# Norms of q and k stacked in one tile, and small matmuls over fewer contraction rows, in a decoder trunk on one core

## The chip, the cores and the metric

The kernel runs on one core of a Trainium2 chip. The metric is the device time of one execution in microseconds; the time of a kernel is the median of several runs.

## The reference

One inference step of a four-layer decoder trunk, for a prompt of 256 positions and 8 sample sequences of 4 positions: 288 columns in all, model width 1024. Each layer is `x += FFN/2; x += Mixer(RMSNorm(x)); x += FFN/2`; the mixers are RWKV-7 (layers 0 and 3), differential attention (layer 1) and gated DeltaNet (layer 2). What matters here is how norms per head are used:

```
def l2norm(t, eps):
    return t * lax.rsqrt(jnp.sum(t * t, axis=-1, keepdims=True) + eps)
...
    q = l2norm(qkv_c[..., :H * DK].reshape(B, T, H, DK), 1e-6) * (DK ** -0.5)
    k = l2norm(qkv_c[..., H * DK:2 * H * DK].reshape(B, T, H, DK), 1e-6)
...
    o = rmsnorm(o, p['norm_w']) * jax.nn.silu(z.astype(f32).reshape(B, T, H, DV))
```

RWKV-7 normalises its key per head of 64 and its output per head (mean and variance); attention and DeltaNet normalise their output per head of 128. Attention adds a bias that depends on the distance of query and key, from a table of 32 buckets.

## The kernel before

Activations lie with features on partitions: eight pieces of 128 features (`CH` = 8) by 288 columns (`NT`). Weights stream through a ring of four slots. Large products are made in three reduced-precision products (`three_products`, lines 911 to 913: high by high, low by high, high by low), 8 x 3 = 24 matmuls per piece of 128 output features; ScalarE makes the high part of a weight piece, VectorE the low part. Each engine has its own hand-written program; semaphores order them, and `after(s)` waits for the next count of one.

A norm per head is made in four steps. TensorE sums squares over the features of a head with a 0/1 matrix as weights (`heads64` or `heads128`, 16 columns: two rows per head of 128, one per head of 64), accumulating over the pieces into 16 rows of a bank. ScalarE takes the root into `rms`. VectorE takes the reciprocal into `rinv`. TensorE spreads the 16 rows of `rinv` over 128 partitions again with the 0/1 matrix `spread64`, 128 columns per piece, and VectorE multiplies. Before the change the spreading matmul contracts over all 128 partitions; `spread64` is zero below row 16.

Where this stands:
- RWKV output norm: line 1210 spreads, VectorE's lines 2795 and 2797 use the result piece by piece.
- RWKV key norm: `own_rows` builds 16 rows (line 2803 on VectorE for the first chunk, 3279 on GpSimd for the others), line 1228 spreads them with `parity`, five times a stage, between the chunk's other matmuls.
- `head_norms` (lines 1835 and 1845): output norm of attention and DeltaNet. Between the two, `keep_clock` runs two matmuls on a constant.
- DeltaNet, `gdn`: the loop over c = 0 to 31 makes q, k, v and the gate. Behind the 24 products of each c from 8 to 23 stands one sum-of-squares matmul (line 1651): j = 0 to 7 for q into bank 7, j = 8 to 15 for k into bank 6, each into 16 rows. Behind c = 25, 26 and 27 stand 6, 6 and 4 spreading matmuls (line 1660), j < 8 from `rinv` and j >= 8 from `kinv`, into banks 4 to 7 in turn; from j = 4 on each waits until VectorE (line 3073) has used the bank. ScalarE takes the two roots (2395, 2396), VectorE the two reciprocals (3067, 3068), the second of which releases TensorE.
- Attention, samples' bias: line 1471 (33 rows by 8 columns), then eight matmuls of line 1475 from `rel_rows` and the one-hot `sample{i}`, both zero below row 33, then page transposes (line 1487).

A float32 matmul appears in the trace as two records, each with its weight load (PEld).

Of the kernel before, what the change touches and what calls it, by code (L numbers as in the profile page):

```python
# [8 lines left out]
DEC_B, DEC_T = 8, 4  # L9
NS = DEC_B * DEC_T  # L10
NT = SEQ + NS
CH = D // 128
# [20 lines left out]
def constant_table():  # L33
# [49 lines left out]
    wide = np.arange(CH * 128)[None, :]  # L83
    put("spread64", (np.arange(RH)[:, None] == wide // DE))
    put("heads128", (np.arange(94)[None, :] // 2 == 23) & (m >= 0))
# [56 lines left out]
def program(nc, t, stages):  # L142
# [5 lines left out]
    with ctx:  # L148
        def sb(name, shape, dt=f32):
            return ctx.enter_context(nc.sbuf_tensor(name, shape, dt))  # L150
# [47 lines left out]
        prm = sb("prm", [128, 512])  # L198
        kinv = sb("kinv", [128, NT])
        banks = ctx.enter_context(nc.psum_tensor("banks", [128, 8, 512], f32))  # L200
# [116 lines left out]
        def W(i):  # L317
            return work[:, i]
# [65 lines left out]
        MK_BANK, MB_BANK = ((6, 7), (2, 3)), ((3, 0), (0, 1))  # L384
        own_inverse = work[:, XM0_, :, :].rearrange("p c n -> p (c n)")

# [183 lines left out]
        pageT = [atok_flat[:, 1024 * i:1024 * i + 1024] for i in range(2)]  # L570
        rel_rows = atok_flat[:, REL_AT:REL_AT + 1024].rearrange("p (a i r) -> p a i r", a=2, i=DEC_T)
        q_apart = atok_flat[:, REL_AT + 1024:REL_AT + 3072].rearrange("p (h b n) -> p h b n", h=AH, b=DEC_B)
# [300 lines left out]
        def _(pe):  # L873
            pe.sem_inc(half_done, 2 * SLOTS)

            pe.wait_ge(first_in, 32)
            pe.wait_ge(consts_set, 5)
            nc.tensor.transpose(bank[0][:, 0:N_NORM], prm_rows[0:N_NORM, 0, :], ident[0:N_NORM, 0:N_NORM]).then_inc(prm_transposed, 1)
# [95 lines left out]
            def rwkv(s, j):  # L974
# [232 lines left out]
                for c in range(CH):  # L1207
                    if c >= 5:
                        after(og_ready)
                    nc.tensor.matmul(bank[OUT_SPREAD_BANK[c]][:, 0:NT], const("spread64")[:, 128 * c:128 * c + 128], rinv[:, :],  # L1210
                                     start=True, stop=True).then_inc(mean_raw, 1)
# [13 lines left out]
            def spread_inverse(i):  # L1225

                t, n, own = own_part(i)
                nc.tensor.matmul(bank[SPREAD_BANK[i]][:, 0:CH * n], const("parity"), own,
                                 start=True, stop=True).then_inc(rk_sum, 1)
# [215 lines left out]
            def attention(s):  # L1445
# [27 lines left out]
                for a in range(2):  # L1473
                    for i in range(DEC_T):
                        last = nc.tensor.matmul(bank[(7, 5)[a]][:, 0:SK], rel_rows[:, a, i, :], acon_at(f"sample{i}"),
                                                start=(i == 0), stop=(i == DEC_T - 1))
                    last.then_inc(sbias_raw, 1)
# [130 lines left out]
            def gdn(s):  # L1608
# [23 lines left out]
                for c in range(32):  # L1632
# [14 lines left out]
                    if 8 <= c < 24:  # L1647
                        j = c - 8
                        at = 46 - 2 * (j % 8)
                        after(qk_squared)  # L1650
                        last = nc.tensor.matmul(bank[7 - j // 8][0:RH, 0:NT], const("heads128")[:, at:at + RH], W(GO_)[:, j % 8, :],
                                                start=(j % 8 == 0), stop=(j % 8 == 7), skip_group_check=True)
                        if j == 15:
                            last.then_inc(qk_ssq, 1)
                    if c == 25:
                        after(qk_ready)
                    for j in {25: range(0, 6), 26: range(6, 12), 27: range(12, 16)}.get(c, ()):
                        if j >= 4:
                            after(qk_ready)
                        nc.tensor.matmul(bank[4 + j % 4][:, 0:NT], const("spread64")[:, 128 * (j % 8):128 * (j % 8) + 128],  # L1660
                                         (rinv, kinv)[j // 8][:, :], start=True, stop=True).then_inc(ks_raw, 1)
                    if c in (28, 29):
# [168 lines left out]
            def head_norms(src, at, spread_bank, meanwhile=lambda: None):  # L1831

                for c in range(CH):
                    after(sub_squared)
                    last = nc.tensor.matmul(bank[at][0:RH, 0:NT], const("heads128")[:, 46 - 2 * c:62 - 2 * c], W(src)[:, c, :],
                                            start=(c == 0), stop=(c == CH - 1))
                last.then_inc(sub_ssq, 1)
                meanwhile()
                keep_clock(spread_bank[0], 2)
                after(sub_rms)  # L1840
                after(og_ready)
                for c in range(CH):
                    if spread_bank[c] in spread_bank[:c]:
                        after(og_ready)
                    nc.tensor.matmul(bank[spread_bank[c]][:, 0:NT], const("spread64")[:, 128 * c:128 * c + 128], rinv[:, :],
                                     start=True, stop=True).then_inc(mean_raw, 1)
# [167 lines left out]
        def _(act):  # L2014
# [61 lines left out]

            act.wait_ge(consts_set, 5)
            after = follow(act)
# [250 lines left out]
            def gdn(s):  # L2329
# [64 lines left out]
                after(qk_ssq)  # L2394
                nc.scalar.activation(rms[0:RH, :], bank[7][0:RH, 0:NT], ACT.Sqrt, bias=eps_col[0:RH, 0:1])
                nc.scalar.activation(kinv[0:RH, :], bank[6][0:RH, 0:NT], ACT.Sqrt, bias=eps_col[0:RH, 0:1]).then_inc(qk_rms, 1)
                convolved(23)
# [123 lines left out]
        def _(dve):  # L2521
# [278 lines left out]
            def own_rows(i):  # L2800

                t, n, own = own_part(i)
                return TT(own[0:RH].rearrange("p (c n) -> p c n", n=n), rinv[0:RH, t].unsqueeze(1).broadcast_to([RH, CH, n]),
                                         const("own_head", RH).unsqueeze(2).broadcast_to([RH, CH, n]), ALU.mult)
# [54 lines left out]
            def attention(s):  # L2859
# [24 lines left out]
                for q in range(8):  # L2884
# [3 lines left out]
                    if q == 2:  # L2888
# [6 lines left out]
                        link(V.memset(rel_rows, 0.0))  # L2895
                        rr = rel_rows[0:BUCKETS + 1].rearrange("p a i (h b q) -> p a i h b q", h=4, b=DEC_B)
                    if q == 4:
# [92 lines left out]
            def gdn(s):  # L2990
# [75 lines left out]
                after(qk_rms)  # L3066
                V.reciprocal(rinv[0:RH, :], rms[0:RH, :])
                V.reciprocal(kinv[0:RH, :], kinv[0:RH, :]).then_inc(qk_ready, 1)

# [205 lines left out]
        def _(pool):  # L3275
            def own_rows(i):

                span, n, own = own_part(i)
                return nc.gpsimd.tensor_tensor(own[0:RH].rearrange("p (c n) -> p c n", n=n),
                                               rinv[0:RH, span].unsqueeze(1).broadcast_to([RH, CH, n]),  # L3280
                                               const("own_head", RH).unsqueeze(2).broadcast_to([RH, CH, n]), ALU.mult)
# [3 lines left out]
            for i, e in enumerate((EPS, 1e-24, 64e-5, 1e-5)):  # L3285
                nc.gpsimd.memset(eps_col[:, i:i + 1], e).then_inc(consts_set, 1)
            nc.gpsimd.memset(kinv[:, :], 1.0).then_inc(consts_set, 1)
            for src, i0, k, p0, n in row_loads[1:]:
# [275 lines left out]
```

## Time and profile before

| | |
|---|---|
| median of 3 runs | 2921.92 us (2921.31 to 2927.31) |
| the profiled execution | 2921.92 us, its span 2920.2 us |
| mean granted TensorE clock | 0.986 of full speed |
| TensorE matmuls busy | 2814.5 us, 96% of the span |
| VectorE busy | 1699.9 us, 58% |
| ScalarE busy | 1176.5 us, 40% |
| GpSimd busy | 255.5 us, 9% |

Times of a place are microseconds from the start of the span. A matmul's duration in a record includes its latency; matmuls follow each other faster than that, so starts tell the pace. The DeltaNet stage lies between about 1630 and 1919 us, attention between 996 and 1190, the RWKV stages between 245 and 560 and between 2365 and 2680.

### The profile page before, as it was taken

How to read it: one execution, taken by the hardware profiler on the slowest of the kernel's cores; microseconds unless marked ns; L12 is line 12 of the kernel's file. 1: busy time of each engine (PE TensorE's matmuls, PEld its weight loads, DVE VectorE, ACT ScalarE, POOL GpSimd, SP SyncE). 2: the span in 40 equal slices, each digit the busy share in tenths (PEclk: the TensorE clock that was granted, in tenths of full speed). 3: DMA queues.
4: the chain of work that ended last, by engine and by line, in shares of the span. 5: the costliest groups of instructions: out<-in, count | busy, mean ns of one | idle time of the engine just before them, and what ended most of it. 6: DMA issues, size and time to landing. Idle time of an engine off the chain costs nothing.

```text
span 2920.2 us, 63483 instructions
## 1 busy us (share of the span) xinstructions
PE 2814.5 (96%) x28153; PEld 2615.4 (90%) x28153; DVE 1699.9 (58%) x2572; ACT 1176.5 (40%) x1835; POOL 255.5 (9%) x334
## 2 busy tenths in 40 slices
PE   7999988999999997999999998999999999889998
PEld 7997778899999985999999888789999977788997
DVE  5646465765565546765564674456556465656654
ACT  4434333444444334544443563234344343334442
POOL 1001011100000201000000110410000010111001
PEclk9999999999999998999999999899999999999999
DMA  7443401553644654444544433254454444115531
GB/s 249 148 143 126 155 8 33 149 172 119 204 154 136 238 188 174 144 155 144 185 145 134 155 125 93 67 173 147 143 186 154 141 150 133 14 33 149 166 126 56
DMA packets 349205, 402.68 MB, mean 138 GB/s; under 512 B 31210, under 2 KB 303999, under 8 KB 348573
## 3 DMA queue, kind: packets, MB, share of 16 engines
q1 hardware_dynamic: 337696, 360.58, 38.6%
q0 software_dynamic: 11312, 39.25, 4.4%
q8 instruction: 151, 2.47, 0.4%
q14 instruction: 46, 0.38, 0.0%
HBM read 385.22 MB, written 14.57 MB: 137 GB/s over the span
## 4 chain that ended last, share of the span: by engine, by line
PE 88%; DVE 8%; ACT 2%; issue 1%; DMA 1%; POOL 0%; SPq 0%; DVEq 0%; ACTq 0%; POOLq 0%
PE banks L911 23%; PE banks L913 22%; PE banks L912 22%; PE banks L944 2%; PE banks L1077 2%; PE banks L1318 2%; PE banks L1290 1%; PE banks L1025 1%; DVE h L2539 1%; PE banks L1914 1%; PE banks L1782 1%; PE banks L901 1%; PE banks L1487 1%; PE banks L1399 1%; PE banks L1333 0%
## 5 line engine op out<-in xcount | busy, mean ns | idle before, releaser
L2554 DVE TENSOR_TENSOR w_lo<-ring,w_hi 128x2048 fp32r<-128x2048 f32 (+1 forms) x304 | 611.5, 2012 | 412.3 <-ACT w_hi L2085 412.1
L911 PE MATMUL banks<-h_hi,w_hi 128*128 128x288 f32 x2816 | 837.8, 298 | 7.4 <-DVE h_lo L2546 6.8
L912 PE MATMUL banks<-h_hi,w_lo 128*128 128x288 f32 x2816 | 831.7, 295 | 0.0
L913 PE MATMUL banks<-h_lo,w_hi 128*128 128x288 f32 x2816 | 828.8, 294 | 0.0
L2085 ACT CAST w_hi<-ring 128x2048 fp32r<-128x2048 f32 (+1 forms) x304 | 511.4, 1683 | 586.2 <-PE banks L913 555.8
L911 PEld LDWEIGHTS banks<-h_hi,w_hi 128*128 128x128 f32 x2816 | 528.4, 188 | 10.6 <-issue 6.1
L913 PEld LDWEIGHTS banks<-h_lo,w_hi 128*128 128x128 f32 x2816 | 531.4, 189 | 0.0
L912 PEld LDWEIGHTS banks<-h_hi,w_lo 128*128 128x128 f32 x2816 | 529.7, 188 | 0.4
L911 PE MATMUL banks<-hid_hi,w_hi 128*128 128x288 f32 x1408 | 416.1, 296 | 0.0
L912 PE MATMUL banks<-hid_hi,w_lo 128*128 128x288 f32 x1408 | 415.4, 295 | 0.0
L913 PE MATMUL banks<-hid_lo,w_hi 128*128 128x288 f32 x1408 | 414.3, 294 | 0.0
L913 PEld LDWEIGHTS banks<-hid_lo,w_hi 128*128 128x128 f32 x1408 | 265.1, 188 | 0.0
L912 PEld LDWEIGHTS banks<-hid_hi,w_lo 128*128 128x128 f32 x1408 | 264.3, 188 | 0.0
L911 PEld LDWEIGHTS banks<-hid_hi,w_hi 128*128 128x128 f32 x1408 | 263.9, 187 | 0.0
L2503 ACT CAST hid_hi<-work 128x288 fp32r<-128x288 f32 x176 | 76.1, 433 | 398.2 <-DVE work L3247 398.2
L3298 POOL TENSOR_TENSOR h<-h 128x288 f32<-128x288 f32 x65 | 80.4, 1237 | 1719.0 <-ACT h L2038 918.4
L3240 DVE TENSOR_TENSOR work<-banks,rinv 128x288 f32<-128x288 f32 x176 | 80.4, 457 | 155.5 <-PE banks L913 155.5
L912 PE MATMUL banks<-h_hi,ring_lo 128*128 128x288 f32 x448 | 133.4, 298 | 0.0
L3249 DVE TENSOR_TENSOR hid_lo<-work,hid_hi 128x288 fp32r<-128x288 f32 x176 | 80.7, 458 | 87.9 <-ACT hid_hi L2503 87.9
L944 PE MATMUL banks<-work,ring 128*128 128x288 f32 x384 | 94.0, 407 | 0.5 <-DVE work L3204 0.5
L944 PEld LDWEIGHTS banks<-work,ring 128*128 128x128 f32 x384 | 72.7, 190 | 20.9 <-DVE work L3204 1.0
L912 PEld LDWEIGHTS banks<-h_hi,ring_lo 128*128 128x128 f32 x448 | 85.6, 191 | 0.2
(582 smaller groups left out, 4143.9 us busy)
## 6 DMA issues: line engine op xcount, KB each, us to landing
ring<-in_ffn_w_gate SPq DMA_DIRECT2D x88, 1024.0 KB, 5.5
ring<-in_ffn_w_up SPq DMA_DIRECT2D x88, 1024.0 KB, 8.0
ring<-in_ffn_w_down SPq DMA_DIRECT2D x64, 768.0 KB, 4.7
ring<-in_ffn_w_down SPq DMA_DIRECT2D x64, 640.0 KB, 5.9
ring<-in_rwkv_w_rkv SPq DMA_DIRECT2D x24, 1024.0 KB, 6.7
ring<-in_gdn_w_in SPq DMA_DIRECT2D x16, 1024.0 KB, 6.9
ring<-in_attn_w_qkv SPq DMA_DIRECT2D x12, 1024.0 KB, 7.3
ring<-in_rwkv_w_o SPq DMA_DIRECT2D x8, 1024.0 KB, 6.2
```

The lines of the kernel that those rows point to most:

```text
L911: nc.tensor.matmul(out, w_hi_k, x_hi_k, start=start, stop=False)
L912: nc.tensor.matmul(out, w_lo_k, x_hi_k, start=False, stop=False)
L913: return nc.tensor.matmul(out, w_hi_k, x_lo_k, start=False, stop=stop)
L944: last = nc.tensor.matmul(bank[(d0 + d) % 8][:, 0:NT], w[:, k, 128 * (d % 4):128 * (d % 4) + 128], src[:, k, :], start=(k == 0), stop=(k = ...
L1077: last = nc.tensor.matmul(bank[d % 4][:, 0:NT], w[:, k, 128 * (d % 4):128 * (d % 4) + 128], W(XM1_)[:, k, :], start=(k == 0), stop=(k == C ...
L1318: last = nc.tensor.matmul(bank[(XT_BANK if w else XY_BANK)[g]][to, 64 * q:64 * q + 64], y if w else xt, xt if w else y, start=True, stop=True)
L2085: nc.scalar.copy(w_hi[e][:, 0:k, :], raw).then_inc(w_hi_ready, 1)
L2503: nc.scalar.copy(hid_hi[:, 2 * u + e, :], prod[:, e, :]).then_inc(act_hi_ready, 1)
L2554: nc.vector.tensor_tensor(w_lo[e][:, 0:k, :], raw, w_hi[e][:, 0:k, :], ALU.subtract).then_inc(w_lo_ready, 1)
L3240: nc.vector.tensor_tensor(silu[:, e, :], bank[2 * e][:, 0:NT], rinv[:, :], ALU.mult)
L3249: nc.vector.tensor_tensor(hid_lo[:, f, :], prod[:, e, :], hid_hi[:, f, :], ALU.subtract).then_inc(act_lo_ready, 1)
L3298: nc.gpsimd.tensor_tensor(h[:, c, :], h[:, c, :], h[:, other, :], ALU.add).then_inc(presummed, 1)
```

## The change

In DeltaNet the sums of squares of q and k go into one bank, q's in rows 0 to 15, k's in rows 32 to 47: all sixteen matmuls of line 1651 have 48 columns of weights and form one accumulation. One root and one reciprocal over 48 rows replace two of each over 16, and the tile `kinv` with its initial fill is gone. `spread64` holds its pattern a second time from row 32. The spreading matmuls read 16 rows of weights and of `rinv`: from row 0 for q, from row 32 for k.

The other matmuls with zero rows are cut to the rows that hold something: 16 for the output norms (1210, 1845) and `parity` (1228), 33 for the samples' bias (1475).

```diff
-    put("spread64", (np.arange(RH)[:, None] == wide // DE))
+    put("spread64", (np.arange(48)[:, None] % 32 == wide // DE))
...
-        kinv = sb("kinv", [128, NT])
...
-        own_inverse = work[:, XM0_, :, :].rearrange("p c n -> p (c n)")
+        own_inverse = work[0:RH, XM0_, :, :].rearrange("p c n -> p (c n)")
...
-        rel_rows = atok_flat[:, REL_AT:REL_AT + 1024].rearrange("p (a i r) -> p a i r", a=2, i=DEC_T)
+        rel_rows = atok_flat[0:BUCKETS + 1, REL_AT:REL_AT + 1024].rearrange("p (a i r) -> p a i r", a=2, i=DEC_T)
...
-                    nc.tensor.matmul(bank[OUT_SPREAD_BANK[c]][:, 0:NT], const("spread64")[:, 128 * c:128 * c + 128], rinv[:, :],
+                    nc.tensor.matmul(bank[OUT_SPREAD_BANK[c]][:, 0:NT], const("spread64", RH)[:, 128 * c:128 * c + 128], rinv[0:RH, :],
...
-                nc.tensor.matmul(bank[SPREAD_BANK[i]][:, 0:CH * n], const("parity"), own,
+                nc.tensor.matmul(bank[SPREAD_BANK[i]][:, 0:CH * n], const("parity", RH), own,
...
-                        last = nc.tensor.matmul(bank[(7, 5)[a]][:, 0:SK], rel_rows[:, a, i, :], acon_at(f"sample{i}"),
+                        last = nc.tensor.matmul(bank[(7, 5)[a]][:, 0:SK], rel_rows[:, a, i, :], acon_at(f"sample{i}", BUCKETS + 1),
...
-                        at = 46 - 2 * (j % 8)
+                        at = 46 - 32 * (j // 8) - 2 * (j % 8)
                         after(qk_squared)
-                        last = nc.tensor.matmul(bank[7 - j // 8][0:RH, 0:NT], const("heads128")[:, at:at + RH], W(GO_)[:, j % 8, :],
-                                                start=(j % 8 == 0), stop=(j % 8 == 7), skip_group_check=True)
+                        last = nc.tensor.matmul(bank[7][0:48, 0:NT], const("heads128")[:, at:at + 48], W(GO_)[:, j % 8, :],
+                                                start=(j == 0), stop=(j == 15), skip_group_check=True)
...
-                        nc.tensor.matmul(bank[4 + j % 4][:, 0:NT], const("spread64")[:, 128 * (j % 8):128 * (j % 8) + 128],
-                                         (rinv, kinv)[j // 8][:, :], start=True, stop=True).then_inc(ks_raw, 1)
+                        r = slice(32 * (j // 8), 32 * (j // 8) + RH)
+                        nc.tensor.matmul(bank[4 + j % 4][:, 0:NT], const("spread64")[r, 128 * (j % 8):128 * (j % 8) + 128],
+                                         rinv[r, :], start=True, stop=True).then_inc(ks_raw, 1)
...
-                    nc.tensor.matmul(bank[spread_bank[c]][:, 0:NT], const("spread64")[:, 128 * c:128 * c + 128], rinv[:, :],
+                    nc.tensor.matmul(bank[spread_bank[c]][:, 0:NT], const("spread64", RH)[:, 128 * c:128 * c + 128], rinv[0:RH, :],
...
-                nc.scalar.activation(rms[0:RH, :], bank[7][0:RH, 0:NT], ACT.Sqrt, bias=eps_col[0:RH, 0:1])
-                nc.scalar.activation(kinv[0:RH, :], bank[6][0:RH, 0:NT], ACT.Sqrt, bias=eps_col[0:RH, 0:1]).then_inc(qk_rms, 1)
+                nc.scalar.activation(rms[0:48, :], bank[7][0:48, 0:NT], ACT.Sqrt, bias=eps_col[0:48, 0:1]).then_inc(qk_rms, 1)
...
-                V.reciprocal(rinv[0:RH, :], rms[0:RH, :])
-                V.reciprocal(kinv[0:RH, :], kinv[0:RH, :]).then_inc(qk_ready, 1)
+                V.reciprocal(rinv[0:48, :], rms[0:48, :]).then_inc(qk_ready, 1)
...
-            nc.gpsimd.memset(kinv[:, :], 1.0).then_inc(consts_set, 1)
```

TensorE and ScalarE wait for four counts of `consts_set` instead of five. The fill of `rel_rows` covers its 33 rows.

## Rows read from the trace of the kernel before

**Rows 1.** The page, chain that ended last: share of the span by engine.

```profile
PE 88%; DVE 8%; ACT 2%; issue 1%; DMA 1%; POOL 0%; SPq 0%; DVEq 0%; ACTq 0%; POOLq 0%
```

**Rows 2.** The chain in order of time, DeltaNet, 1734 to 1775: start, us, what.

```profile
1739.84 1.13 DVE ring_lo L2996
1740.98 1.85 DVE rinv L3067
1742.83 1.82 DVE kinv L3068
1744.70 0.77 PE banks L1660 x2
```

**Rows 3.** Timeline, 1735 to 1775: start, us, what, in brackets idle before and releaser.

```profile
1740.19 0.48 ACT L2396 ACTIVATE kinv<-banks,eps_col 16x288 f32<-16x288 f32 x1
...
1742.84 0.29 PE L913 MATMUL banks<-h_lo,gdn_w_hi 128*128 128x288 f32 x1
...
1744.69 2.24 PEld L1660 LDWEIGHTS banks<-rinv,consts 128*128 128x128 f32 x10 [1.80 <-DVE kinv L3068]
```

**Rows 4.** Timeline, 1757 to 1760, the four spreads behind c = 27.

```profile
1757.21 0.29 PE L913 MATMUL banks<-h_lo,gdn_w_hi 128*128 128x288 f32 x1
...
1757.34 2.10 PE L1660 MATMUL banks<-kinv,consts 128*128 128x288 f32 x8
...
1759.41 0.29 PE L912 MATMUL banks<-h_hi,ring_lo 128*128 128x288 f32 x1
```

**Rows 5.** Groups by form, VectorE: line, operation, form, count, busy us, mean ns.

```profile
L2532 DVE RECIPROCAL rinv<-rms 128x288 f32<-128x288 f32 x13 | 25.4, 1951 | 12.4 <-ACT rms L2031 12.3
```

**Rows 6.** Timeline of TensorE's weight loads, 270 to 273.5, line 1025.

```profile
271.49 0.78 PEld L1025 LDWEIGHTS banks<-work,ring 128*128 128x128 f32 x4 [0.38 <-ACT work L2139]
272.66 0.30 PEld L1025 LDWEIGHTS banks<-work,ring 32*128 32x128 f32 x4 [0.39 <-ACT work L2141]
273.34 0.30 PEld L1025 LDWEIGHTS banks<-work,ring 64*128 64x128 f32 x4 [0.39 <-issue]
```

**Rows 7.** Timeline of TensorE, 1676.2 to 1678, one sum of squares.

```profile
1676.37 0.29 PE L913 MATMUL banks<-h_lo,gdn_w_hi 128*128 128x288 f32 x1
1676.59 0.66 PE L1651 MATMUL banks<-work,consts 128*16 128x288 f32 x2
...
1677.42 0.30 PE L912 MATMUL banks<-h_hi,ring_lo 128*128 128x288 f32 x1
```

**Rows 8.** The chain in order of time, attention, 1015 to 1030.

```profile
1021.08 4.08 PE banks L1475 x16
1025.16 1.75 PE banks L1487 x16
```

**Rows 9.** The chain in order of time, attention, 1160 to 1180.

```profile
1169.91 4.12 PE banks L1845 x16
1174.03 3.18 PE banks L956 x24
```

**Rows 10.** Timeline of TensorE, 1895 to 1899; the chain, RWKV, 532 to 545.

```profile
1896.45 2.94 PE L944 MATMUL banks<-work,ring 128*128 128x288 f32 x11 [0.55 <-DVE work L3204]
...
535.60 0.46 DVE work L2797
536.05 0.38 DVE work L2795
```

**Rows 11.** Groups by form, weight loads of 16, 32 and 64 columns.

```profile
L1651 PEld LDWEIGHTS banks<-work,consts 128*16 128x16 f32 x32 | 1.8, 94 | 2.6 <-issue 2.6
L1012 PEld LDWEIGHTS banks<-work,ring 128*32 128x32 f32 x32 | 1.8, 110 | 0.0
L992 PEld LDWEIGHTS banks<-work,ring 128*64 128x64 f32 x64 | 8.3, 136 | 8.2 <-issue 2.2 <-DVE work L2630 1.2
```

**Rows 12.** Timeline of GpSimd, 0 to 12.

```profile
1.17 0.34 POOL L3287 MEMSET kinv<- 128x288 f32 x1
```

**Rows 13.** Windows, TensorE: window, length, busy (count), granted clock, DMA share, GB/s.

```profile
267.10:279.40 12.30, 12.18 (x67) 1.00 0.50 171
1163.20:1167.20 4.00, 3.98 (x17) 1.00 0.00 0
1785.30:1792.20 6.90, 6.00 (x123) 0.51 0.66 191
1850.20:1853.60 3.40, 3.40 (x30) 0.51 1.02 295
```

More of the change, by code:

```diff
@@ L876, in _ @@
             pe.wait_ge(first_in, 32)
-            pe.wait_ge(consts_set, 5)
+            pe.wait_ge(consts_set, 4)
             nc.tensor.transpose(bank[0][:, 0:N_NORM], prm_rows[0:N_NORM, 0, :], ident[0:N_NORM, 0:N_NORM]).then_inc(prm_transposed, 1)
@@ L2075, in out_high @@
                         high_part(unit_base[s + 1], c // 2 - 2)
-            act.wait_ge(consts_set, 5)
+            act.wait_ge(consts_set, 4)
             after = follow(act)
@@ L2802, in own_rows @@
                 t, n, own = own_part(i)
-                return TT(own[0:RH].rearrange("p (c n) -> p c n", n=n), rinv[0:RH, t].unsqueeze(1).broadcast_to([RH, CH, n]),
+                return TT(own.rearrange("p (c n) -> p c n", n=n), rinv[0:RH, t].unsqueeze(1).broadcast_to([RH, CH, n]),
                                          const("own_head", RH).unsqueeze(2).broadcast_to([RH, CH, n]), ALU.mult)
@@ L2895, in attention @@
                         link(V.memset(rel_rows, 0.0))
-                        rr = rel_rows[0:BUCKETS + 1].rearrange("p a i (h b q) -> p a i h b q", h=4, b=DEC_B)
+                        rr = rel_rows.rearrange("p a i (h b q) -> p a i h b q", h=4, b=DEC_B)
                     if q == 4:
@@ L3278, in own_rows @@
                 span, n, own = own_part(i)
-                return nc.gpsimd.tensor_tensor(own[0:RH].rearrange("p (c n) -> p c n", n=n),
+                return nc.gpsimd.tensor_tensor(own.rearrange("p (c n) -> p c n", n=n),
                                                rinv[0:RH, span].unsqueeze(1).broadcast_to([RH, CH, n]),
```

## The prediction

> **What bounds the kernel now.** I began with the last chain of the page: TensorE holds 88% of it, VectorE 8% [rows 1]. An edit counts, then, where it moves TensorE's next instruction. The change touches small matmuls between the big products, so I went from the chain to each of its places and asked: is TensorE waiting there, or are its matmuls back to back?
>
> In the delta-rule stage it waits once. After the 24 products of c = 25 the chain leaves TensorE: VectorE takes the reciprocal of q's norms (1740.98 us, 1.85 us) and of k's (1742.83, 1.82), and only then do the spreading matmuls start, at 1744.70 [rows 2]. Their weight load sat 1.80 us behind the k reciprocal; the product before them started at 1742.84, and with the products' pitch of 0.13 us TensorE could have gone on at 1742.97 [rows 3]. So the hole is 1744.70 - 1742.97 = 1.73 us. Later, at c = 27, matmuls of the same line have no hole: last product 1757.21, first spread 1757.34, and after eight records the second product of c = 28 at 1759.41 [rows 4]. (One float32 matmul is two records.) Taking off the slot of one product, the eight fill 1757.34 to 1759.28, 0.2425 us each, nothing lost on entering or leaving.
>
> **The wait that goes.** One root over 48 rows replaces two over 16. ScalarE loses a 0.48 us activation [rows 3]; VectorE's first reciprocal starts behind its own split of weights (1739.84, 1.13 us), not behind the second root [rows 2, 3], so this is worth nothing at that point. The second reciprocal goes. One over 128 rows takes 1.95 us [rows 5] against 1.85 on the chain for 16 [rows 2], so 48 rows cost what 16 do. It is ready at 1742.83, and TensorE's load followed the old one's end at once: ready about 1742.9, just before TensorE needs it. The whole 1.73 us goes, and what is late next is TensorE itself. Everything behind is on the chain or waits for it, so it shifts along. **-1.73.**
>
> **The price of another shape in the array.** The change also cuts the rows that matmuls contract over: 16 instead of 128 for the spreads, 33 for the samples' bias. Does a shape change cost? In the RWKV stage one line runs in groups of 128, 32 and 64 rows: its weight loads begin at 271.49, 272.66 and 273.34 [rows 6]. The 128-row group is two matmuls, four records: 4 x 0.2425 = 0.97 of 1.17 us, 0.20 over. The 32-row group has two matmuls in two different row strips, which can overlap: 0.68 = 2 x 0.2425 + 0.20. So I take 0.20 us per change of shape. A second place agrees roughly: the 16-column matmuls between products take from 1676.50 (1676.37 + 0.13) to 1677.29 (1677.42 - 0.13), 0.79 us for 0.485 of work, 0.30 for entering and leaving [rows 7]. I take the larger. The lower bound is zero, as in [rows 4], should contraction rows not count as a shape.
>
> The Trainium skill, "TensorEngine Tiling (Array Packing)", Key Properties, speaks against this edit: changing the tiling mode drains TensorE. It gives no price; from the lone-matmul latency of "TensorE: Matmul & The Clock Gate", Single matmul latency, 398 extra cycles at 2.4 GHz, I get an estimate of 0.166 us a change, so 1.33 instead of 1.60 us in the sum below.
>
> Where new shape changes are on the chain:
> - spreads at c = 25, 26, 27: three entries, three exits. Rows 0 to 15 and 32 to 47 are one shape in two strips. 6 x 0.20 = **+1.20**. At c = 26, j = 7 and j = 8 are in different strips and banks; one matmul's record may hide: **-0.24** (bounds 0 and -0.49).
> - attention, samples' bias: its eight matmuls run straight into the transposes [rows 8]; it was entered from a 33x8 shape already. One exit: **+0.20**.
> - attention's head norms: the 16 records run straight into the output projection [rows 9]. The entry lies in the wait for the reciprocal. One exit: **+0.20**.
> - hidden: after the delta-rule head norms TensorE waits 0.55 us for VectorE [rows 10], which covers 0.20; without that cover it would be +0.20. In both RWKV stages the spreads are paced by VectorE, whose two operations per piece fill the time (0.46 + 0.38) [rows 10]; without it, +0.20 a stage. The five `parity` matmuls a stage stand between shapes of 64 rows or columns, so no change is added.
>
> **The wider norm sums.** Sixteen matmuls go from 16 to 48 columns. The load of 16 columns takes 94 ns, of 32 110 ns, of 64 136 ns [rows 11]; between the last two, 48 is about 124. The first load of each insertion is exposed, since the shape changes: 16 x 0.03 = **+0.48** (bounds: none exposed 0, both 0.96). The streamed columns stay 288. These products are back to back, so this moves the whole of c = 8 to 25, the reciprocal with it.
>
> **At nothing.** The `kinv` fill on GpSimd (0.34 us at 1.17) [rows 12] is away from TensorE's start, which the first weights set. Fewer semaphore counts, a fill of 33 rows rather than 128, the freed bank and the freed tile move nothing. No DMA is added or moved.
>
> **Sum:** -1.73 + 1.20 - 0.24 + 0.20 + 0.20 + 0.48 = +0.11 us. Ends of the unknowns: shape changes and loads free, -1.73 - 0.49 = -2.2; nothing hidden, both loads exposed, and the three covered exits paid: -1.73 + 1.20 + 0.40 + 0.96 + 0.60 = +1.4. The profiled execution took 2921.92 us around a span of 2920.2, and is also the median. 2921.92 + 0.11 = **2922.0 us**.
>
> **Rivals.**
> *The clock falls in the narrow stretches (slower).* Five stretches of about 4 us (bias, four head norms) would keep one eighth or a quarter of the rows at work. If the granted clock falls to 1.2 GHz after one for the shortest half-clock stretch seen, 3.4 us at 0.51 [rows 13], TensorE loses 1.7 us; five times, 8.5 us: 2930.4. It decides from four on. Against it: 12.3 us of the mixed 64-, 128- and 32-row line, and 4 us with only 16 columns, all at 1.00 [rows 13]. But in the first, strips worked side by side; 16 rows alone for 4 us is not in the trace. 7%. The skill ("TensorE: Matmul & The Clock Gate", Part 1) names busyness as what the gate watches, not rows; by that the clock stays.
>
> *The next weights are not loaded ahead (slower).* In one strip a load might have to wait for the matmul before it: 0.19 us more per record. Paid by 32 records at c = 25 to 27, 16 in the bias, 32 in the attention and delta-rule head norms: 80 x 0.19 = 15.2 us, 2937. It decides from about a third of that. Against it: four 32-row loads, two to a strip, are done in 0.30 us [rows 6]. 4%.
>
> *The clock does better (faster).* The same wait gone, and half-clock stretches behind it shrink, as the one at 1785.3 [rows 13]: 6.9 us at 0.51, a loss of 3.4. The removed hole is not the idle just before it, so I see only the shift of times that may do this. -1.73 and two such, -6.8: with the costs above about 2916. 4%.
>
> *The merge brings what it says, the rows are free (faster by less than can be told).* -1.73 - 0.24 + 0.48 = -1.5: 2920.4. This is inside no change; so are all mixtures. With the forecast, 85%.
>
> **How the numbers follow.** About 0.2%, 5.8 us, is what a measurement of this kernel can tell from no change. Forecast and its near mixtures 85%, slower 11%, faster 4% (the faster case rounded up to 5%, the forecast down to 84%). The range takes the bounds -2.2 and +1.4 and on each side the clock: one half-clock stretch less (-1.7), two more (+3.4): 2918.0 to 2926.7.
>
> **What the changed profile would show.** The reciprocal of 48 rows at 1.9 us and no second; the wait of the c = 25 spreads gone or under 0.3 us. At c = 27, from last product to first spread 0.2 us more than 0.13, and as much on leaving; if these gaps are not there, the shape price fails and the time is nearer 2920. The 48-column loads at about 124 ns, 0.82 us an insertion. The granted clock at 1.00 in all four head norms and the bias; if it is not, the first rival. A pitch of 0.43 in place of 0.24 us in the 16-row records would be the second. Wrong too if VectorE, not TensorE, were late at c = 25 through something I don't see.

## The result, and the profile after

The changed kernel took 2939.36 us (median of 8 runs, 2933.63 to 2949.81), the kernel before 2925.16 in the same session (8 runs, 2920.72 to 2930.21). The ratio is 1.0059, 95% interval 1.0045 to 1.0075: slower. A ratio here and below compares all undisturbed executions on record of both kernels (14 of the changed one), so it need not be the quotient of the two medians, 1.0049 here. The profiled execution took 2942.88 us around a span of 2941.2, 21.0 us more than before, with a mean granted clock of 0.977 (before 0.986). In this version the lines of the change moved by one: products 910 to 912, norm sums 1650, bias 1470 and 1474, output projection 955 and 959; 1660 and 1845 are the same.

The page's chain is still TensorE's, and its share rose from 88% to 89% [rows 1]:

```profile
PE 89%; DVE 7%; ACT 2%; issue 1%; DMA 1%; POOL 0%; SPq 0%; DVEq 0%; ACTq 0%; POOLq 0%
```

So no other engine took over. The first thing to look at is the place where the wait was. The timeline of TensorE around c = 25 (start, us, what, in brackets the idle time before):

```profile
1757.21 0.29 PE L912 MATMUL banks<-h_lo,gdn_w_hi 128*128 128x288 f32 x1
...
1757.43 1.75 PEld L1660 LDWEIGHTS banks<-rinv,consts 16*128 16x128 f32 x8 [0.16 <-issue]
```

The hole of 1.73 us [rows 3] is gone: the last product's slot ends at 1757.21 + 0.13 = 1757.34, and the spreads' first weights load at 1757.43. The change did what it says there. One sum of squares between the products, same view:

```profile
1690.25 0.29 PE L912 MATMUL banks<-h_lo,gdn_w_hi 128*128 128x288 f32 x1
...
1690.48 0.69 PE L1650 MATMUL banks<-work,consts 128*48 128x288 f32 x2
...
1691.33 0.30 PE L911 MATMUL banks<-h_hi,ring_lo 128*128 128x288 f32 x1
```

From 1690.38 to 1691.20 it is 0.82 us, against 0.79 with 16 columns [rows 7]. Both are the sizes of the prediction.

Now the chain in order of time, attention, at the samples' bias and the transposes, and then at the head norms and the output projection:

```profile
1023.41 6.64 PE banks L1474 x16
1030.06 3.60 PE banks L1486 x16
...
1178.90 5.22 PE banks L1845 x16
1184.12 5.40 PE banks L955 x24
```

Before, these four steps took 4.08, 1.75, 4.12 and 3.18 us [rows 8, 9]. The narrow matmuls are longer, and so are the wide ones behind them, which the change doesn't touch. The windows view says why (window, length, TensorE's busy time with the number of its records, granted clock, DMA share, GB/s); first the kernel before at its norms and bias in RWKV, attention, attention, DeltaNet, RWKV:

```profile
533.80:544.00 10.20, 9.68 (x51) 1.00 0.62 202
1021.00:1031.20 10.20, 10.13 (x101) 1.00 0.69 250
1169.90:1176.70 6.80, 6.79 (x38) 1.00 0.00 0
1891.80:1898.60 6.80, 6.25 (x25) 1.00 0.65 186
2653.60:2663.80 10.20, 9.65 (x51) 1.00 0.60 195
```

The changed kernel at the same places, and behind the spreads at c = 25, 26 and 27:

```profile
536.10:542.90 6.80, 6.80 (x22) 0.54 0.70 228
1024.20:1034.40 10.20, 10.20 (x46) 0.53 0.49 187
1181.20:1188.00 6.80, 6.80 (x24) 0.54 0.00 0
1761.50:1764.90 3.40, 3.40 (x18) 0.58 0.02 5
1768.30:1771.70 3.40, 3.40 (x16) 0.58 0.00 0
1775.10:1778.50 3.40, 3.40 (x15) 0.58 1.00 343
1908.20:1915.00 6.80, 6.25 (x16) 0.54 0.31 92
2672.80:2683.00 10.20, 10.20 (x35) 0.53 0.51 167
```

TensorE is busy in all of them and gets through fewer records: 24 against 38 in 6.80 us at the attention norm, 46 against 101 in 10.20 us at the bias. The clock had fallen to its lower level, 1.2 GHz. (These windows begin about 0.5 us ahead of the fall, which is why they read 0.53 to 0.58; moved on by that much, each of them reads 0.50.) The fall comes inside the narrow run and lasts beyond it: the norms' first narrow records start at 534.42, 1178.90, 1905.81 and 2671.45 us, and the clock is at half from 536.6, 1181.8, 1908.8 and 2673.4 on, 1.9 to 3.0 us later. The first rival of the prediction is there, at each of its five places (the bias and the four output norms), and also between and behind the spreads, where the prediction had not looked for it. Where the norms' time went shows in the stretch from each output-norm reciprocal to the next norm's first sum: before 37.25, 34.96, 45.14 and 37.25 us, after 38.95, 38.29, 48.18 and 40.48: +11.3 us. The bias stretch adds 4.35 us (5.90 to 10.25). Together 15.6 of the 21.0 us between the two spans.

The spreads lose time too, and it comes back behind them. Between the groups of c = 25 and 26, and of 26 and 27, the same run of products takes 4.44 us in the changed kernel (1761.32 to 1765.76, 1768.68 to 1773.12) and took 2.90 before (1748.22 to 1751.12). But from there to the DeltaNet norm the kernel before has half-clock stretches of its own, as the one at 1785.3 [rows 13], and the changed kernel has fewer. The windows from c = 28 to the norm's reciprocal, the kernel before, then the changed one:

```profile
1763.00:1889.70 126.70, 116.65 (x2052) 0.91 0.23 67
1779.20:1903.70 124.50, 114.17 (x2065) 0.95 0.23 67
```

From the second product of c = 28 to that reciprocal it is 130.3 us before (1759.41 to 1889.71) and 128.0 after (1775.74 to 1903.72). This is one execution of each.

### The profile page after: what moved, and what is told of

It reads as the page before. It is cut to its first block, busy times and chain, and to the rows that moved or that the text cites. A ratio compares the mean times of both kernels' runs of the same rounds, so it can differ in the third digit from the quotient of the medians.

```text
span 2941.2 us, 63480 instructions
## 1 busy us (share of the span) xinstructions
PE 2838.1 (96%) x28153; PEld 2633.9 (90%) x28153; DVE 1697.8 (58%) x2571; ACT 1176.0 (40%) x1834; POOL 256.6 (9%) x333
## 4 chain that ended last, share of the span: by engine, by line
PE 89%; DVE 7%; ACT 2%; issue 1%; DMA 1%; POOL 0%; SPq 0%; DVEq 0%; ACTq 0%; POOLq 0%
PE banks L910 23%; PE banks L912 22%; PE banks L911 22%; PE banks L943 2%; PE banks L1076 2%; PE banks L1317 2%; PE banks L1289 1%; PE banks L1024 1%; DVE work L2629 1%; DVE work L2721 1%; DVE h L2538 1%; PE banks L1486 1%; PE banks L1914 1%; PE banks L900 1%; PE banks L955 1%
```

## The experiments

Three theories stood at the start. A: few contraction rows lower the clock. B: the changes of shape cost more than 0.20 us. C: the merge itself (wider sums, one reciprocal) costs. All ratios below are to the kernel before on the same chip, with 95% intervals; the median of before was 2922.07, 2922.63, 2924.52 and 2922.55 us in the four sessions.

### First session: the merge apart from the rows, and the number of rows

**merge_full_rows**: the merge alone. Every matmul contracts over 128 rows; k's spread table is built by GpSimd in a free part of `h`.

```
+ if c == 12: memset(hflat[:, 0:1024], 0.0); tensor_copy(hflat[32:48, 0:1024], const("spread64", RH))
- ... const("spread64")[r, 128 * (j % 8):128 * (j % 8) + 128], rinv[r, :]
+ spread = const("spread64")[:, 128 * j:128 * j + 128] if j < 8 else hflat[:, 128 * j - 1024:128 * j - 896]
+ ... spread, rinv[:, :]
```

> The merge alone (norm sums of q and k in one bank, one root, one reciprocal), with every matmul contracting over all 128 rows as before; k's spreads take their 128-row 0/1 matrix from a table that GpSimd builds in a free part of h. Clock theory (few contraction rows lower the granted clock): no new half-clock stretches behind the spreads of c = 25 to 27, the bias and the output norms; the time is 1 to 2 us below the kernel before, which its measurement can hardly tell (ratio 0.999 to 1.001). Rival (the merge itself, its wider sums, costs the time): ratio about 1.006, as with the whole change.

**rows16_all**, **rows64_all**, **rows96_all**: the kernel before with all cut matmuls (norms, spreads, parity, bias) over 16, 64 or 96 rows (the bias 33, 64, 96), no merge.

```
- const("spread64")[:, ...], rinv[:, :]          + const("spread64", R)[:, ...], rinv[0:R, :]
- const("parity"), own                           + const("parity", R), own
- acon_at(f"sample{i}")                          + acon_at(f"sample{i}", max(R, 33))
```

> The row cuts alone, no merge: 16 rows in the spreads, the parity matmuls and the output norms, 33 in the bias. Clock theory: half-clock stretches behind each of the groups, ratio 1.005 to 1.009, as slow as the whole change or slower by the 1 to 2 us that the merge gives. Rival (the merge costs it): ratio 1.000 to 1.001.

> The same matmuls cut to 64 rows instead of 16. The array's shape changes here as with 16 rows. Shape theory (entering and leaving another shape, or loads not made ahead, costs the time): as slow as with 16 rows, ratio 1.005 or more. Clock theory, if the number of rows at work is what counts: clearly less than with 16, ratio under 1.003, fewer or no new half-clock stretches; if any cut of rows does it, as with 16.

> The same matmuls cut to 96 rows. Clock theory by the number of rows: no new half-clock stretches, ratio 0.999 to 1.001. Shape theory: 96 rows need the full shape, so also 0.999 to 1.001; together with the 64-row run this tells whether shape or rows decide. If it is as slow as with 16 rows, both fall.

| kernel | us | ratio | interval |
|---|---|---|---|
| merge_full_rows | 2921.19 | 0.9992 | 0.9983 to 1.0001 |
| rows16_all | 2942.43 | 1.0061 | 1.0048 to 1.0074 |
| rows64_all | 2925.71 | 1.0015 | 1.0006 to 1.0024 |
| rows96_all | 2924.10 | 1.0006 | 0.9997 to 1.0014 |

The merge doesn't cost; theory C falls. The row cuts alone, with nothing else of the change, give all of the loss (1.0061 against 1.0059). At 64 rows most of it is gone. Yet the price of the shape is the same there: at c = 27 of rows64_all, by the reckoning of [rows 4], the eight records fill 2.33 us where it was 1.94, and over 16 rows they fill 2.34 (second session). So B can't be the main cause. In rows64_all the windows over the bias and the first norms read:

```profile
533.80:551.00 17.20, 16.57 (x109) 1.00 0.23 74
1020.00:1035.00 15.00, 14.93 (x188) 1.00 0.79 262
```

In merge_full_rows one reciprocal over 48 rows takes what the prediction said (timeline; 1.95 for 128 rows [rows 5]):

```profile
1744.90 1.94 DVE L3069 RECIPROCAL rinv<-rms 48x288 f32<-48x288 f32 x1
```

### Second session: which place, and 32 rows

Each kernel is the one before with one cut: **rows32_all** as above with R = 32; **only_norms16** the four output norms; **only_spreads16** the spreads at c = 25 to 27; **only_bias33** the bias.

```
only_norms16:   + const("spread64", 16)[:, 128 * c:128 * c + 128], rinv[0:16, :]
only_spreads16: + const("spread64", 16)[:, 128 * (j % 8):...], (rinv, kinv)[j // 8][0:16, :]
only_bias33:    + acon_at(f"sample{i}", 33)
```

> The same matmuls as in the cut to 16 rows, but over 32 rows (the bias stays at 33). The array's shape is the same as with 16 rows, one strip; only the number of rows at work is doubled. Shape theory (one strip of 32, whatever is in it, costs it): ratio 1.005 to 1.007, as with 16. Row-count theory, in proportion: between 16 rows (1.0061) and 64 rows (1.0015), about 1.003 to 1.005.

> The kernel before with only the spreads of the four output norms (two RWKV, attention, gated DeltaNet) cut to 16 rows. Clock theory: a half-clock stretch behind each of the four, none behind the bias and c = 25 to 27; 6 to 12 us, ratio 1.002 to 1.004, the costs of the places adding up to the 18 us of the full cut. Shape theory: four exits of 0.2 us, ratio under 1.001.

> The kernel before with only the spreads at c = 25 to 27 of gated DeltaNet cut to 16 rows (from rinv and kinv, no merge). Three groups of 1.5 to 3 us between full-row products. Clock theory: short half-clock stretches among c = 25 to 28, 2 to 6 us, ratio 1.001 to 1.002. Shape theory: six changes of 0.2 us, 1.2 us, not told from nothing.

> The kernel before with only the samples' bias in attention cut to 33 rows. 33 rows need the 64-row shape. In the changed kernel the clock was at half from inside this group on. If 33 rows are few enough, half clock for 7 to 10 us there, 3 to 5 us, ratio 1.001 to 1.002; if what stood in the full change was set off by something else, nothing, 0.999 to 1.001.

| kernel | us | ratio | interval |
|---|---|---|---|
| rows32_all | 2938.57 | 1.0050 | 1.0037 to 1.0063 |
| only_norms16 | 2936.76 | 1.0047 | 1.0033 to 1.0061 |
| only_spreads16 | 2923.40 | 1.0000 | 0.9991 to 1.0010 |
| only_bias33 | 2927.60 | 1.0018 | 1.0007 to 1.0030 |

The norms are worth 13.7 us (0.47% of 2922.6; by the interval 10 to 18), the bias 5.3 (2 to 9), the spreads nothing that can be measured. For the norms that is more than the clock theory had expected, for the spreads less. 32 rows lie where both theories of that run allow it. The bias in its own kernel, in the windows view:

```profile
1023.50:1030.30 6.80, 6.80 (x38) 0.50 0.41 150
```

The windows of only_norms16 at its four norms show the same fall as the changed kernel:

```profile
539.50:546.30 6.80, 6.78 (x23) 0.55 0.58 186
1177.80:1184.60 6.80, 6.80 (x22) 0.55 0.00 0
1904.80:1911.60 6.80, 6.25 (x16) 0.55 0.39 114
2666.00:2676.20 10.20, 10.20 (x33) 0.53 0.55 181
```

Its four stretches from reciprocal to next norm sum grew by 1.9, 3.4, 3.0 and 3.3 us, 11.6 of the 14.8 us between the spans; the other 3.2 us arose before the first norm, which the edit can't reach.

only_spreads16 gives the price of a shape change without the merge. Timeline at c = 27:

```profile
1758.52 0.29 PE L913 MATMUL banks<-h_lo,gdn_w_hi 128*128 128x288 f32 x1
...
1758.75 0.51 PE L1660 MATMUL banks<-kinv,consts 16*128 16x288 f32 x1
...
1761.12 0.29 PE L912 MATMUL banks<-h_hi,ring_lo 128*128 128x288 f32 x1
```

Eight records fill 1758.65 to 1760.99, 2.34 us, where before it was 1.94 [rows 4]: 0.40 more for entering and leaving, 0.10 of it ahead of the first record. That is the prediction's 2 x 0.20. It also leaves no room for 0.19 us more per record, which would be 1.5 us here: the rival of weights not loaded ahead falls. At c = 26 the twelve records fill 3.31 us, 0.40 more than the 2.91 before; in the changed kernel, where they stand in two strips, they fill 2.66 us at the full clock (1765.76 + 0.13 to 1768.68 - 0.13). So the second strip saves 0.65 us.

### Third session: parity, a repeat, and two attempts to hold the clock

**only_parity16**: `const("parity", 16)` and 16 rows of `own_inverse`, nothing else. **merge_full_again**: merge_full_rows once more. **norms16_filled**: only_norms16 with a 128-row matmul behind each narrow one, whose result nobody reads. The edit reached the two RWKV norms alone; attention and DeltaNet stayed as in only_norms16, which its expectation doesn't say. **change_with_strips4**: the changed kernel, norm sums written in four copies (112 columns), so that the spreads of c = 0, 1, 2, 3 read four row strips in turn; the bias over 128 rows.

```
norms16_filled:
+ nc.tensor.matmul(bank[0][:, 0:NT], ident, consts[:, 0:NT], start=True, stop=True)
change_with_strips4:
+ bank[at][0:112, 0:NT], const("heads4x")[:, 14 - 2 * c:126 - 2 * c]
+ const("spread64")[32 * (c % 4):32 * (c % 4) + RH, ...], rinv[32 * (c % 4):32 * (c % 4) + RH, :]
```

> The kernel before with only the parity matmuls of the RWKV key norm cut to 16 rows: five a stage, 0.5 to 2 us each, far apart. The other three places measured 1.0047, 1.0018 and 1.0000 alone, all four together 1.0061; so this one should be nothing, 0.999 to 1.001, by the clock theory and by the shape theory alike. If it is over 1.002, the parts do not add up and something else acts.

> The merge with all matmuls over 128 rows a second time, since it is the candidate for beating both kernels: 0.9992 [0.9983, 1.0001] the first time. From the trace the wait of 1.73 us at c = 25 goes and the wider loads cost 0.4 to 0.5 us: ratio 0.9995, that is 0.9986 to 1.0004; clearly faster only if the interval stays below 1.

> The cut of the output norms' spreads to 16 rows (1.0047 alone), with one matmul on a constant over all 128 rows and 288 columns behind each narrow one in the two RWKV norms and in attention (not in gated DeltaNet). Its result is overwritten and not used. It adds 8 x 0.49 = 3.9 us of TensorE work per place, which is on the path in attention and almost wholly under VectorE's 0.86 us per piece in RWKV. Clock theory: full clock behind the RWKV and attention norms again, still half behind the DeltaNet norm; about 3.9 + 2 x 1 + 3 = 9 us over the kernel before, so less than with the narrow ones alone: ratio 1.002 to 1.0035. Shape theory: more work and more shape changes, so slower than without it: ratio over 1.006.

> The whole change, but the four output norms' sums are made in four copies (112 columns, rows 0, 32, 64 and 96), the root and reciprocal taken over 112 rows, and the spreads of pieces c and c + 4 read their 16 rows from strip c mod 4, so that up to four run side by side; the bias is back at 128 rows. The merge and the narrow spreads at c = 25 to 27 stay. Theory that few rows at work in the array at one time lower the clock: four times 16 rows is 64 at once, so the clock behind the norms is held or falls less, unless TensorE then idles longer because the spreads are over sooner; ratio 0.999 to 1.002. Theory that the narrow shape as such does it: half clock behind the norms as before, ratio about 1.004.

| kernel | us | ratio | interval |
|---|---|---|---|
| only_parity16 | 2923.19 | 0.9998 | 0.9989 to 1.0007 |
| merge_full_again | 2920.53 | 0.9993 | 0.9982 to 1.0004 |
| norms16_filled | 2954.13 | 1.0099 | 1.0084 to 1.0114 |
| change_with_strips4 | 2935.13 | 1.0036 | 1.0022 to 1.0049 |

Parity costs nothing that can be measured. The merge repeats at 0.9993. The fill was a miss: full-row matmuls in between did not keep the clock up, and the time came out on the shape theory's side (over 1.006). Windows over the two RWKV norms:

```profile
532.70:549.80 17.10, 17.10 (x37) 0.52 0.24 76
2676.20:2696.70 20.50, 20.50 (x45) 0.52 0.24 80
```

The low stretches became longer, 17 and 20 us. Each alternation is two shape changes: one narrow and one full matmul are 0.97 us of records, but such pairs follow each other by 1.33 to 1.36 us at the full clock, and by 2.52 us once it is at half, so that TensorE and no longer VectorE (0.84 us a piece [rows 10]) sets the pace. The changes alone, 16 pairs at 0.40 us, are 6.4 of the 29 us; they don't explain the time without the clock. That full rows are mixed in is not enough; their share over time, or the drains between, may decide, and this run can't say which.

Strips in turn held the clock at the attention norm and at no other. Windows at RWKV, attention, DeltaNet (the second RWKV norm reads 0.50 from 2669.1 to 2675.9):

```profile
536.10:542.90 6.80, 6.80 (x25) 0.53 0.50 158
1174.40:1181.20 6.80, 6.77 (x45) 1.00 0.00 0
1901.40:1908.20 6.80, 6.20 (x14) 0.52 0.19 57
```

In attention the eight spreads stand back to back and the strips overlap: the 16 records start within 2.5 us, where it was 3.7; in RWKV VectorE paces them, and in DeltaNet a wait for VectorE follows [rows 10]. That fits what we see, but was not tested.

### Fourth session: how long a narrow run may be, and the change repaired

**norms_half16**: only the first four of the eight output-norm spreads over 16 rows. **only_norms64**: the output norms over 64 rows. **merge_rows64**: the merge, its q rows in 0 to 15 and its k rows in 64 to 79 (sums of 80 columns), the spreads and the output norms over 64 rows, parity and bias over 128.

```
norms_half16: + const("spread64", RH if c < 4 else 128)[...], rinv[0:RH if c < 4 else 128, :]
only_norms64: + const("spread64", 64)[...], rinv[0:64, :]
merge_rows64:
+ put("spread64", (np.arange(80)[:, None] % 64 == wide // DE))
+ at = 78 - 64 * (j // 8) - 2 * (j % 8)
+ bank[7][0:80, 0:NT], const("heads128")[:, at:at + 80]
+ r = slice(64 * (j // 8), 64 * (j // 8) + 64)
+ const("spread64", 64)[:, 128 * c:128 * c + 128], rinv[0:64, :]
```

> The kernel before with only the first four of the eight spreads of each output norm cut to 16 rows (0.97 us of TensorE work on end at full clock, 2 us with both records), the last four over 128. All eight cut cost 1.0047; full-row matmuls between all the narrow ones, in the RWKV norms, did not hold the clock and cost 1.0099. Theory A (a long narrow run is needed; half of it is too short, as at c = 25 to 27): no half-clock stretch behind, ratio 0.9995 to 1.0010. Theory B (any narrow work next to the waits of a norm tips the clock): half clock behind at least three of the four, ratio 1.002 to 1.005.

> The kernel before with only the output norms' spreads cut to 64 rows. With all places at 64 rows the ratio was 1.0015, with the norms at 16 alone 1.0047. If the number of rows at work decides and 64 is enough: 0.9995 to 1.0010, and no half-clock stretch behind the norms. If the remainder of 1.0015 sits in the norms: 1.001 to 1.002.

> The change repaired: q's norms in rows 0 to 15, k's in rows 64 to 79, one root and one reciprocal over 80 rows, and every spread at c = 25 to 27 and of the output norms contracts over 64 rows; parity and bias are back at 128. Clock theory: no half-clock stretches that the kernel before has not, the wait at c = 25 gone (-1.7 us), the 80-column loads 16 x 0.06 = +0.9, shape changes +1.6: +0.8 us, ratio 0.9995 to 1.0012. Rival (the merge or the strips as such cost it): 1.004 or more.

| kernel | us | ratio | interval |
|---|---|---|---|
| norms_half16 | 2925.35 | 1.0002 | 0.9993 to 1.0011 |
| only_norms64 | 2921.30 | 0.9997 | 0.9986 to 1.0009 |
| merge_rows64 | 2917.06 | 0.9985 | 0.9976 to 0.9995 |

Four narrow spreads in a row cost nothing that can be measured, eight cost 13.7 us over four norms: the loss isn't in proportion to the number of narrow matmuls, nor does it go with the shape changes (norms_half16 has as many as only_norms16). The windows of norms_half16 at RWKV, attention, DeltaNet and RWKV:

```profile
533.80:551.00 17.20, 15.78 (x94) 1.00 0.39 123
1169.00:1190.00 21.00, 20.27 (x127) 1.00 0.01 1
1893.00:1905.00 12.00, 10.91 (x37) 0.86 0.45 128
2655.00:2675.00 20.00, 18.57 (x106) 1.00 0.36 113
```

The clock held at three norms; at the DeltaNet norm it was at half for 3.4 us (from 1896.8). In only_norms64 the windows at all four norms read 1.00. merge_rows64 is faster than both kernels, by an interval that ends at 0.9995. Its windows over bias, attention norm, merged spreads and DeltaNet norm:

```profile
1020.00:1035.00 15.00, 14.15 (x151) 1.00 0.68 220
1165.00:1185.00 20.00, 19.27 (x108) 1.00 0.00 1
1740.00:1760.00 20.00, 19.47 (x119) 1.00 0.30 97
1885.00:1905.00 20.00, 18.90 (x103) 1.00 0.30 86
```

And the place of the old wait, in its timeline: the reciprocal, then the spreads' weights.

```profile
1737.93 1.94 DVE L3066 RECIPROCAL rinv<-rms 80x288 f32<-80x288 f32 x1
...
1739.92 2.23 PEld L1660 LDWEIGHTS banks<-rinv,consts 64*128 64x128 f32 x10 [0.29 <-DVE rinv L3066]
```

Of the 1.80 us [rows 3], 0.29 are left. But the three groups of spreads, wait and shape changes taken together, fill 9.2 us against 10.0 before, and the medians lie 5.5 us apart (4.4 by the ratio). Most of that is in the norm sums, which the expectation had at +0.9 us. One of them, TensorE's timeline:

```profile
1692.56 0.29 PE L912 MATMUL banks<-h_lo,gdn_w_hi 128*128 128x288 f32 x1
1692.69 0.65 PE L1650 MATMUL banks<-work,consts 128*80 128x288 f32 x2
...
1693.31 0.29 PE L911 MATMUL banks<-h_hi,ring_lo 128*128 128x288 f32 x1
```

With 80 columns of weights it takes 0.49 us (1692.69 to 1693.18), against 0.79 with 16 [rows 7] and 0.82 with 48: nothing is lost on entering or leaving. Sixteen times 0.30 is 4.8 us. So the price of 0.30 that [rows 7] shows is one that weights of 16 and of 48 columns pay and weights of 80 don't. With the 0.8 us of the spreads that is 5.6 us, which is the gain; it needs no help from the clock. Its profiled execution, whose span of 2912.1 is 8.1 below the one of before, is the fastest of its twelve. The merge with 80 columns and all spreads over 128 rows was not run.

## Why the prediction was wrong

The prediction said 2922.0 us with a range to 2926.7 and "no change" at 84%. It came out at 2939.36 us and a ratio of 1.0059, slower and outside the range. By its own steps:

- **The wait that goes (-1.73): right.** The hole is gone, and the reciprocal over 48 rows takes 1.94 us. (The 1.80 us of [rows 3] are the idle time that the k reciprocal ended, and not a distance behind it; the 1.73 don't rest on them.) With the 48-column loads, -1.73 + 0.48 = -1.25 us; the merge alone measured 0.9992 and 0.9993, some -2 us, each interval reaching just past 1.
- **The wider sums (+0.48): right** for 48 columns. Loads of 120 ns (estimated 124), 0.82 us an insertion, as said. That 80 columns would cost 0.49 it could not see, having no row of such a shape.
- **A shape change at 0.20 us: right in sum,** 0.40 a pair, though split 0.10 and 0.30 between entry and exit and not 0.20 each, and the same over 64 rows. The Trainium skill ("TensorEngine Tiling (Array Packing)", Key Properties) says that a change of mode drains TensorE; this trace agrees, with 0.40 us a pair, and the 0.33 estimated from the Trainium skill's latency would be a little low.
- **The two strips at c = 26 (-0.24, bounds 0 and -0.49): too small.** It measured -0.65, beyond the bound.
- **Weights not loaded ahead: refuted** by the time of the eight records at c = 27 in only_spreads16.
- **Parity, `kinv`'s fill, semaphores, at nothing: right** as far as measured (parity 0.9998; the fill and the semaphores went with the merge, 0.9992 and 0.9993).
- **The faster rival, half-clock stretches behind the hole that shrink: there, but not as a gain.** In the changed kernel's profile they did shrink (0.91 to 0.95 up to the DeltaNet norm), and this only made up for the new ones among the spreads. (Its sum, by its own terms, is 2915, not 2916.)
- **The clock: the step that failed.** The sum has no term for it: the forecast took the granted clock to stay at 1.00 at the norms and the bias. The runs showed half clock there, 17 us by the ratio. The prediction had this mechanism as its first rival, "the clock falls in the narrow stretches", with 7% and 8.5 us. Two parts of it were wrong.

The first is the weighing of the evidence. "4 us with only 16 columns, all at 1.00" [rows 13] was read as evidence that a sparsely used array keeps the clock. But those matmuls contract over 128 rows. Columns and rows are different dimensions, and what the runs show concerns rows: 16, 32, 64 and 96 of them gave 1.0061, 1.0050, 1.0015 and 1.0006. The other row, the mixed line of 64, 128 and 32 rows, held strips side by side and full rows; the prediction itself noted that "16 rows alone for 4 us is not in the trace", and still gave that case only 7%. A case that no row shows should get the chance of something unknown, and not the one that rows of another kind suggest. The Trainium skill ("TensorE: Matmul & The Clock Gate", Part 1) has the gate watch how busy TensorE is. Here, at the attention norm, TensorE counts as busy for 6.79 of 6.80 us before and 6.80 after, at 1.00 and 0.54: the busy time that the profile shows doesn't tell the two kernels apart; the rows do.

The second is the size. The prediction took the shortest low stretch seen, 3.4 us, for each of five places: 1.7 us lost at each. The low stretches were 6.8 or 10.2 us at the norms and the bias, two and three times that, and three more of 3.4 us stood behind c = 25, 26 and 27. The eight make 51 us at half clock; half of it is lost if all of it is TensorE's own pace: up to some 25 us, against 21.0 in the spans and 17 in the ratio (0.59% of 2922).

By parts: norms 13.7 us, bias 5.3, spreads and parity 0, merge -2: 17.0 us, which is the 17 of the ratio, closer than the intervals of the parts promise. The 0 of the spreads is a balance: in the changed kernel's profile they lose 1.5 us between two groups each, and as much comes back up to the DeltaNet norm; in only_spreads16 one stretch of 3.4 us fell (0.50 from 1747.3), and the time stayed at 1.0000; in rows16_all's profile it was one of 10.2 us (from 1763.3). Why the later stretches shrink isn't shown.

The zeros themselves are not what lowers the clock: before, the same 112 rows of weights were zero, and it was 1.00. What counts in these runs is how many rows the matmul contracts over, also where the added rows hold nothing but zero weights. Other contents were not run.

What stays open: why four strips in turn held the clock in attention only; why the fill made the low stretches longer; how the length of a narrow run counts (four matmuls of 16 rows held the clock at three norms of four, while of eight it fell 1.6 to 3.2 us after the first in only_norms16); and the 0.15% of rows64_all, 4.4 us, which isn't in the norms (only_norms64, 0.9997) and of which shape changes at 0.20 us explain about 1.6.

## What to carry to other kernels

Zero rows in a small matmul can be worth keeping: cutting the contraction from 128 rows to 16 left the pace of the matmuls as it was (0.65 us were saved at the one place where two strips worked side by side), cost 0.40 us a run in shape changes, and in runs of about 4 us halved the clock from inside the run until past its end; 64 rows kept it. When a change thins out what the array does, look at the granted clock of the wide work behind each place, because the loss shows there and not in the changed lines alone. Take the gain apart from its wrapping: one norm in place of two is good (-1.73 us of waiting). And measure the neighbouring sizes: the repair with 64-row strips is faster than both kernels, at 0.9985 of before (0.9976 to 0.9995), mostly because its norm sums are 80 columns wide and so lose nothing between the big products (-4.8 us), which no expectation had.

## What was unexpected of the hardware

- TensorE, busy without a break, was granted 1.2 GHz from 1.6 to 3.2 us after the first of eight matmuls (16 records) of 16 contraction rows, and 2.4 GHz through eight of 64 rows, or through four of 16 at three norms of four.
- At the bias of 33 rows the clock fell to 0.50 as well (1.0018); over 64 rows it stayed at 1.00. And 32 rows cost nearly what 16 do (1.0050 and 1.0061).
- A full-row matmul behind every narrow one did not hold the clock: 0.52 over 17.1 and 20.5 us.
- A small matmul between big ones takes 0.79 us with 16 columns of weights, 0.82 with 48 and 0.49 with 80.
- A reciprocal of 288 columns takes the same over 16, 48, 80 and 128 rows: 1.93, 1.94, 1.94 and 1.95 us.
